# The down projection of both layers as one straight stretch of TensorE products, in place of a hardware loop of two halves

## The reference, cut to what matters

```python
D_MODEL = 2048
D_FF = 5632
...
    gate, val = jnp.split(y, 2, axis=-1)
    return (jax.nn.silu(gate) * val) @ w_down
```

## Time and profile before

| what | us |
|---|---|
| median of 3 runs (2253.96, 2254.34, 2261.76) | 2254.34 |
| the profiled execution | 2253.26 |
| its span, first to last instruction | 2251.5 |
| lying around the span | 1.76 |

### The profile page before, as it was taken

The page is one execution under the profiler, slowest core; times in us unless marked ns, Lnnn a source line. Parts: engine busy times, 40 slices in busy tenths (PEclk is TensorE's granted clock), DMA queues, the critical chain, the costliest instruction groups (busy, mean ns, idle before and its releaser), DMA issues.

```text
span 2251.5 us, 47051 instructions
## 1 busy us (share of the span) xinstructions
PE 2231.6 (99%) x17202; PEld 2125.4 (94%) x17202; DVE 1614.0 (72%) x2397; ACT 1216.0 (54%) x1585; POOL 52.0 (2%) x78
## 2 busy tenths in 40 slices
PE   8999999999999999999999999999999999999999
PEld 6888889999999999999988888899999999999899
DVE  8777877888888888555577677777767676665454
ACT  7777765655555555444465577655444444443333
POOL 1111100000000000000000000000000000000000
PEclk9999999999999999999999999999999999999999
DMA  7555555555555555555545554555555555556553
GB/s 232 180 178 185 185 179 194 191 193 195 189 195 196 194 187 196 195 182 196 197 158 191 170 178 168 171 191 194 193 193 191 194 191 192 195 199 202 171 198 131
DMA packets 118634, 422.51 MB, mean 188 GB/s; under 512 B 13773, under 2 KB 15973, under 8 KB 118544
## 3 DMA queue, kind: packets, MB, share of 16 engines
q1 hardware_dynamic: 114048, 413.66, 55.3%
q0 software_dynamic: 2048, 5.42, 1.0%
q10 hardware_dynamic: 2448, 2.11, 0.3%
HBM read 419.01 MB, written 3.70 MB: 188 GB/s over the span
## 4 chain that ended last, share of the span: by engine, by line
PE 99%; issue 0%; DVE 0%; DMA 0%; ACT 0%; SPq 0%; ACTq 0%
PE acc L455 21%; PE acc L452 21%; PE acc L458 21%; PE acc L427 17%; PE acc L436 8%; PE acc L424 3%; PE b_val L424 2%; PE acc L433 2%; PE b_val L433 1%; PE b_score L511 0%; PE b_turn L516 0%; DMA xres<-xt 0%; PE b_mean L524 0%; PE b_score L510 0%; PE b_mean L504 0%
## 5 line engine op out<-in xcount | busy, mean ns | idle before, releaser
L786 ACT ACTIVATE w<-raw 128x1024 fp32r<-128x1024 f32 x783 | 825.4, 1058 | 810.6 <-PE acc L458 615.3
L1097 DVE TENSOR_TENSOR w<-raw,w 128x1024 fp32r<-128x1024 f32 x783 | 959.9, 1229 | 392.1 <-ACT w L786 389.4
L427 PE MATMUL acc<-xs,w 128*128 128x512 f32 x1396 | 368.6, 397 | 1.2 <-DVE xs L1120 1.2
L452 PE MATMUL acc<-xs,w 128*128 128x256 f32 x2436 | 342.1, 276 | 0.0
L455 PE MATMUL acc<-xs,w 128*128 128x256 f32 x2436 | 342.1, 276 | 0.0
L458 PE MATMUL acc<-xs,w 128*128 128x256 f32 x2436 | 342.1, 276 | 0.0
L458 PEld LDWEIGHTS acc<-xs,w 128*128 128x128 f32 x2436 | 306.3, 188 | 0.0
L452 PEld LDWEIGHTS acc<-xs,w 128*128 128x128 f32 x2436 | 306.3, 188 | 0.0
L455 PEld LDWEIGHTS acc<-xs,w 128*128 128x128 f32 x2436 | 306.3, 188 | 0.0
L1103 DVE TENSOR_REDUCE folded_t<-acc 128x256 f32<-128x512 f32 x324 | 223.1, 689 | 112.3 <-PE acc L458 86.4
L427 PEld LDWEIGHTS acc<-xs,w 128*128 128x128 f32 x1396 | 248.1, 188 | 44.5 <-DVE w L1097 1.5
(11 more groups left out here) (223 smaller groups left out, 1852.9 us busy)
## 6 DMA issues: line engine op xcount, KB each, us to landing
raw<-wstream SPq DMA_DIRECT2D x783, 512.0 KB, 3.3
decay_row<-decay_scratch POOLq DMA_DIRECT2D x16, 128.0 KB, 3.6
out<-xres ACTq DMA_DIRECT2D x16, 128.0 KB, 2.8
xres<-xt SPq DMA_DIRECT2D x3, 512.0 KB, 6.3
dist_scratch<-bias_scratch POOLq DMA_DIRECT2D x8, 192.0 KB, 4.6
toeplitz<-dist_scratch POOLq DMA_DIRECT2D x8, 128.0 KB, 3.8
xres<-xt SPq DMA_DIRECT2D x2, 256.0 KB, 3.6
raw<-wstream SPq DMA_DIRECT2D x2, 256.0 KB, 4.2
```

The source lines that it names most:

```text
L427: pe.matmul(acc[bank_no][:, :], w_hi, x[:, kc, :, :].rearrange("p a s -> p (a s)"), start=opens, stop=False)
L452: pe.matmul(acc[bank_no][:, 0:S], w_hi, x[:, kc, 0, :], start=opens, stop=False)
L786: act.activation(whi[slot][:, :], raw[slot][:, :], ACT.Copy).then_inc(hi_ready, 1)
L1097: dve.tensor_tensor(wlo[slot][:, :], raw[slot][:, :], whi[slot][:, :], ALU.subtract).then_inc(lo_ready, 1)
```

## The change

`down` no longer loops. The 704 blocks of a layer are one list, and the counts waited for are constants. SETTLE stands once at the head; 113 groups of six blocks in thirds follow, and one of eight. The 18 blocks that opened the second half are now in thirds like their neighbours. Which blocks are multiplied, in which order, into which banks, and when slots and banks come free is as before. VectorE's, ScalarE's, GpSimd's and SyncE's lists have the same instructions in the same order.

```diff
             def down(layer):
 
-                with pe.Fori(0, 2) as i:
-                    pos = Pos(layer.unit_down, U_DOWN // 2, i)
-
-                    pe.wait_ge(hid_split, FC * (layer.n + 1) - 1)
-                    blocks = []
-                    for b in range(BLOCKS * U_DOWN // 2):
-                        c, kc = divmod(b, FC)
-                        free = layer.chunk_down + 8 * i + c - 3 if kc == 0 else None
-                        late = (hid_split, FC * (layer.n + 1)) if b == FC - 1 else None
-                        blocks.append((b // BLOCKS, b % BLOCKS, c % 4, kc, kc == 0, kc == FC - 1, free, late))
-                    stretch(pos, blocks, hid2, *SETTLE, *[Thirds(6)] * 55, Thirds(4))
+                pos = Pos(layer.unit_down)
+                pe.wait_ge(hid_split, FC * (layer.n + 1) - 1)
+                blocks = []
+                for b in range(BLOCKS * U_DOWN):
+                    c, kc = divmod(b, FC)
+                    free = layer.chunk_down + c - 3 if kc == 0 else None
+                    late = (hid_split, FC * (layer.n + 1)) if b == FC - 1 else None
+                    blocks.append((b // BLOCKS, b % BLOCKS, c % 4, kc, kc == 0, kc == FC - 1, free, late))
+                stretch(pos, blocks, hid2, *SETTLE, *[Thirds(6)] * 113, Thirds(8))
```

## The result

The straight list takes 2238.34 us, the median of four runs (2237.73 to 2240.13); the kernel before took 2258.05 in its four (2253.96 to 2262.06). The ratio is 0.9914, with a 95% interval of 0.9889 to 0.9939: faster by 0.6 to 1.1%. Of the four runs before, two lie near 2254 and two near 2262. The profiled execution took 2238.12 us with a span of 2236.3, 15.14 and 15.2 us less than the profile of before.

What follows compares the result with a forecast made beforehand. TensorE, busy 2231.6 of 2251.5 us, was taken to bound the kernel. Gains of 3.10 (layer 0) and 12.49 us (layer 1), 15.6 together, off 2253.26 gave 2237.7, off the median 2238.7; forecast 2238, range 2235 to 2247.

Steps and rivals of the forecast that it cites:

- The stops are the loop's head being fetched: Middle of both down projections: the 8.3-packet loop has lost its head when it branches back; longest branch 4752 ns.
- Layer 0, 3.10 us: Second half of layer 0's down projection: 119.68 us without the loop in place of 122.78, a gain of 3.10 us.
- (a): Middle of layer 1's down projection: TensorE stops, starts four products, stops again for 2.14 us; 8.03 us together with (b).
- (b): Start of layer 1's second down half: the clock fell to 1.2 GHz, so SETTLE runs slowly; 8.03 us together with (a).
- (c): Rest of layer 1's second down half: products step at 117.8 ns where layer 0's had 113.3; 4.45 us, other bound 0.
- the wide step: Layer 1's second down half: 117.8 ns a product; rival that it stays for another reason, 2242.1 us, chance 0.10.
- a broken start: Reason given for (c): the wide step goes with the stops at the half's start, not with the second half as such.
- What costs nothing: Down projections: 18 blocks changing form (0.04 us to the good), 51 register operations beside products, weights asking for no more.
- The sum: Both down projections: 3.10 + 12.49 = 15.6 us off the profiled 2253.26.
- No packet stopped `up` of layer 1: Rival: layer 1's `up` is fetched anew, 2.9 to 8.0 us a stop; chance 0.07 once, 0.03 each turn.
- the extra one that I expected: Layer 1's `up` loop, moved by the longer list: its branch lies just behind a fifth packet end, where it crossed four.
- The straight list kept the narrow step: Rival: the straight list falls into the wide step earlier, 9.4 us from one layer's head, 2247 us; chance 0.05.

Runs made afterwards that it cites:

- e4: The kernel before, loops kept, with a hint for the back edge (`hint_back_edge=True`) on the down loop: 2239.07 us, ratio 0.9926.
- e2: The kernel before, loops kept, padded so that the down loop's head lies at instruction 0 of a packet in both layers: 2249.02 us, ratio 0.9968.
- e3: The kernel before, loops kept, padded so that the down loop's head lies at instruction 239 of a packet of 256: 2255.39 us, ratio 1.0008.
- e10: The kernel before, unchanged, profiled once more: 2259.7 us.
- e1: The kernel before with layer 0's down projection made straight, layer 1's keeping the loop: 2243.58 us, ratio 0.9954.
- e6: The straight list, in thirds between the halves, with a wait for data put there in each layer: 2260.45 us, a single run.
- e7: The straight list with the same waits for data between the halves as e6, and SETTLE behind each: 2256.95 us, a single run.
- e8: The kernel before, its down loop's body given a second SETTLE in the middle: 2252.91 us, a single run.
- e9: The kernel before with layer 1's down projection made straight, layer 0's keeping the loop: 2243.13 us, ratio 0.9945.
- e5: The straight list with SETTLE also at the head of the second half, as the loop had it: 2239.93 us, ratio 0.9931.

## Why the prediction was right, point by point

- **The stops are the loop's head being fetched.** Right, and shown: with the late fetch gone and everything else left (e4) the time is the straight list's; with the head moved by padding (e2, e3) the second stop goes from layer 1 and comes to layer 0. The Trainium skill, "Runtime: NRT & Kernel Launch", section "Instruction fetch mechanics", says that a taken branch whose target is not held waits until it is fetched. The runs agree: 4752 ns, and at most 396 where the late packet is gone. Its sentence that the window holds two blocks is not what the trace shows, where the returns of `up`, over 4.5 packets, take 208 ns.
- **Layer 0, 3.10 us.** Right against the profile that it was worked out from: 883.34 to 1122.73 is 239.39 us, where 239.4 was forecast. As a price of the loop it was the mild case: in e10 the same stop cost 128.86 - 119.7 = 9.2 us. The sum was worked out from a profile without that fall, though a run of 2261.76 us lay beside it. That the medians lie 19.7 us apart and the two profiles 15.1 is in part the draw: half of the four runs before were near 2262, and the nineteen of before in the batch of e1 to e4 have a median of 2255.34.
- **Layer 1, (a) and (b), 8.03 us.** Right: nothing is left of either. The head's place, 11 instructions before the end of a packet, holds up: 15 instructions more (e1) took the second stop away, and a head put 17 before the end (e3) stopped layer 0 after 17 instructions.
- **Layer 1, (c), 4.45 us, the term without a bound.** The size was right, and so was the link to the stops: no half without a fall of the clock has the wide step. The reason, "a broken start", was vague, and the runs only narrow it. A stop with a fall and no SETTLE behind it left it in both layers (e6). SETTLE did not prevent it in layer 0 of e2, e3, e7, e8 and e10, nor in layer 1 before, although its last pair ran at the full clock there (six products of 512 columns in 1.39 us to the next row, 1.38 being usual):

```profile
2127.60 1.55 PE L427 MATMUL acc<-hid,w 128*128 128x512 f32 x6
```

It was narrow where two whole pairs were left at 2.4 GHz (e3 and e7, layer 1) and behind a second, undisturbed SETTLE (e8); but it was narrow in layer 0 of e9 too, where less was left than in e10. So a fall of the clock goes before the wide step, but which step follows a fall is not settled. Why the step has two lengths at one clock stays open.

- **What costs nothing.** Right: the form of the 18 blocks (e5, 0.01 us a half), the register operations (e4), the weights (197 against 192 and 204 against 177 GB/s, no wait).
- **The sum.** 15.6 was forecast and 15.14 came. The straight kernel's down projection began at 883.34, 0.49 us later than before, ahead of anything that the change touches.
- **The rivals.** No packet stopped `up` of layer 1; the extra one that I expected did come, a turn later than I placed it, and cost nothing. The straight list kept the narrow step.

## What to carry to other kernels

Here a loop of TensorE with a body of 8.3 packets paid for its head at its return, and one of 4.5 packets did not; where between them the bound lies, no run shows. Look for idle time put down to "issue", and for a branch whose duration is in microseconds. Before unrolling, try the hint of e4: here it was worth the same, with some 4100 instructions less in TensorE's list. And price a stop of TensorE by what follows it, the time at the low clock and the step behind, since 4.7 us of waiting cost 11 us.

## What I had not expected of the hardware

- A stop of about 2.8 to 3 us is sometimes followed by a fall of the granted clock and sometimes not, in the same kernel at the same place: in layer 0, not in two profiles of before, but in the one of e10. The straight list has no stop there; its four runs lie within 2.4 us, nineteen of before within 10.8.
- At a granted clock of 1.00 a stream of 256-column products, each with its weight load, ran at 113.3 or at 117.8 ns a step for more than 100 us. Every wide step had a fall of the clock before it, but not every fall left one.
- A hint of 42 ns at the head of the body brought the returning branch from some 4.5 us to at most 0.4 us.
